# Third and fourth probability tile of thirteen attention heads turned in 32x32 blocks by VectorE and by a trip through memory, instead of by TensorE

## The chip, the cores and the metric

One core of one Trainium2 chip. The metric is device time in microseconds (us), from one launch to its end. The profile names the engines PE (TensorE, matrix products), PEld (its weight loads), DVE (VectorE), ACT (ScalarE), POOL (GpSimd) and SP (SyncE, whose queue issues most DMAs).

## The reference

Two layers of a chunk-causal encoder run over 512 prompt tokens and, with the same weights, over 64 sample tokens that also read 128 cached positions. Layer 0 has 8 heads of latent attention (heads 0 to 7 of the kernel) and 8 heads of differential attention (heads 8 to 15: two softmax maps, the second subtracted with a learned factor). Layer 1 has 8 heads of sparse attention over selected keys (heads 16 to 23). A SwiGLU follows each layer. What matters for the change is the last line of each attention:

```
p = jax.nn.softmax(logits, axis=-1)
attn = (p[:, 0] - lam * p[:, 1]).astype(v.dtype)
return jnp.einsum('bhqk,bkhd->bqhd', attn, v)
```

The softmax needs the queries on partitions and the keys along the free axis; the product with the values contracts over keys, so each tile of probabilities has to be turned until its keys lie on partitions.

## The kernel before, in words

Everything is float32, split into a high part (float32r, made by ScalarE with a Copy) and a low part (source minus high part, made by VectorE or POOL); each product is done as high x high, high x low, low x high. Each engine has an instruction stream of its own, written out by hand; the streams meet at semaphores, and a small planner only numbers the events. An attention head is eight slots, s = 0 to 7. In slots 0 to 4 TensorE makes the scores of the five query tiles t = 0 to 4 (tile t < 4 has 128 rows and 128(t+1) keys, tile 4 is the sample group), DVE adds the bias and takes the row maxima (`row_maxima`), ACT exponentiates (`exponents`, L2335) and scales (`scale_probs`, L2343), and in heads 8 to 15 DVE mixes the two maps (`mix_maps`, L3083) in the slot after. In slots 2 to 6 the tile s-2 is turned:

- `turn_probs` (L1712, L1715) on TensorE: t+1 transposes of 128x128 against the identity into one of two PSUM halves T;
- `turned_hi` (L2351) on ACT: high part from PSUM into PTh;
- `turned_lo` (L3090) on DVE: low part into PTl, which frees the PSUM half.

`weighted_values(h)` (L1724 to L1731) reads PTh and PTl of head h in slot 1 of head h+1. All other TensorE work of the slots is filler from other heads: projections of the head after (L1444 with XGh, XGl) and output products of finished heads (L1444 with MIXh, MIXl). Odd heads 9 to 15 carry eight output tiles, and end later; heads 22 and 23 have no projections left, so that head 22 is short.

The order of POOL's stream at the end of a head is: slot 4, low part of the values (Vl) and in odd sparse heads of an output (MIXl, L3652); slot 5, low part of the next keys (Kl, L3652); slot 6, a DMA of cached values (L3735), four DMAs of bias (`load_bias`, L3717, not in heads 14, 15, 22, 23), in sparse heads low part of the next queries (Ql), then the low part of the weight unit begun in this slot (`begin`, L3645); slot 7, such a weight unit if one is due; and after slot 7 of heads 10, 12 and 14 the low parts of the two finished heads' outputs (two MIXl), which TensorE needs for `output_tile` of the next head's slot 0. 

The SP queue issues the loads of weight units (L1090, each waits until its buffer's low part was made), the cached keys (L1149, in slot 2, which waits for the turn of the cached keys at the end of the head before), and in slot 4 the store of the head's keys (`store_keys`, L1133: eight DMAs from KF, which DVE has transposed in 32x32 blocks, L3022) and values. At the end of layer 0 stands a norm during which TensorE has little to do.

Of the kernel before, what the change touches and what calls it, by code (L numbers as in the profile page):

```python
# [144 lines left out]
def early_output(h):  # L145


    return h - 1 if h % 2 and kind_of(h) == "dsa" else None

# [166 lines left out]
def build(nc, a, outs, scratch):  # L316
# [58 lines left out]
    def plan_attention(h):  # L375
# [5 lines left out]
        for s in range(SLOTS):  # L381
# [5 lines left out]
            if 2 <= s < 2 + TOK_TILES and (h, s) != (16, 6):  # L387
                tr.add("p", h, s - 2)
# [333 lines left out]
    with ctx:  # L722
# [103 lines left out]
        assert e <= own  # L826
        (QIh, QIl), end3 = overlay(end3, ("QIh", [P, 4, NT], F32R), ("QIl", [P, 4, NT], F32R))
# [80 lines left out]
        pt_hi = sem("pt_hi")  # L908
        b_sq, rb_sqrt = sem("b_sq"), sem("rb_sqrt")
# [115 lines left out]
        def _(sp):  # L1025
# [112 lines left out]

            def load_next(*place):
# [11 lines left out]
            def attention(h):  # L1151
                x = next_head(h)
                for s in range(SLOTS):
                    if s == 2 and h not in (7, 16) and x is not None and kind_of(x) != "mla":
                        load_cached_keys(x)
                    if s == 4 and kind_of(h) != "mla":
                        store_keys(h)
                    load_next("slot", h, s)

# [268 lines left out]
        def _(pe):  # L1428
# [289 lines left out]
            def weighted_values(h):  # L1718
                out = open_pair("pv", h)
                pe.wait_ge(t_free, tr.made("p", h, QT))  # L1720
                pe.wait_ge(job_lo, jobs.made("v", h))
                for j in range(QT):
                    for part, (v, p) in enumerate(((Vh, PTh), (Vh, PTl), (Vl, PTh))):
                        pe.matmul(out[:, j * P:SEQ], v[:, j, :], p[:, j, j * P:SEQ],  # L1724
                                  start=(j == 0 and part == 0), stop=(j == QT - 1 and part == 2), skip_group_check=True)


                for j, tile in enumerate((TOK_TILES - 1, TOK_TILES)):
                    pe.matmul(out[:, SEQ:NT + DEC], Vh[:, tile, :], PS[:, j, :, :].rearrange("p a q -> p (a q)"),
                              start=(j == 0), stop=False, skip_group_check=True)  # L1730
# [58 lines left out]
            def attention(h):  # L1789
                g, x = prepared_in(h), next_head(h)  # L1790
                for s in range(SLOTS):
# [12 lines left out]
                    if 2 <= s < 2 + TOK_TILES and (h, s) != (16, 6):  # L1804
                        turn_probs(h, s - 2)
# [396 lines left out]
        def _(act):  # L2202
# [123 lines left out]
            def exponents(h, t):  # L2326
                kind, r, w = kind_of(h), rows_of(t), keys_of(t)
                n = step_of(h, t)
                if n >= 2:
                    act.wait_ge(t_done, tr.made("p", *divmod(n - 2, TOK_TILES)))  # L2330
# [24 lines left out]

            def b_square(h):
# [11 lines left out]
            def attention(h):  # L2368
                g, x, p = prepared_in(h), next_head(h), finished_pair(h)
                for s in range(SLOTS):  # L2370
# [6 lines left out]
                    if 2 <= s < 2 + TOK_TILES and (h, s) not in ((15, 5), (16, 4)):  # L2377
                        turned_hi(h, s - 2)
                    if h in OUTPUT_FIRST and s == 2:
# [50 lines left out]
                    if h < 16 and g is not None and s == k_job_slot(g) == 5:  # L2430
                        job("k", g)
                    if s == 5 and h < 7 and h % 2 and h > 1:
# [357 lines left out]
        def _(dve):  # L2790
# [294 lines left out]

            def turned_lo(h, t):
# [71 lines left out]
            def attention(h):  # L3158
                g, x, p = prepared_in(h), next_head(h), finished_pair(h)
                for s in range(SLOTS):  # L3160
# [3 lines left out]
                    if s < TOK_TILES:  # L3164
                        row_maxima(h, s)
                    if h == 16 and s < 3:
# [12 lines left out]
                    if 2 <= s < 2 + TOK_TILES:  # L3179
# [457 lines left out]
        def _(pool):  # L3637
# [15 lines left out]

            def add_squares(norm):
# [89 lines left out]
            def attention(h):  # L3744
                g, x, p = prepared_in(h), next_head(h), finished_pair(h)
                for s in range(SLOTS):
# [282 lines left out]
```

## Time and profile before

| | us |
|---|---|
| median of 3 runs | 1643.68 |
| lowest and highest | 1642.51, 1647.01 |
| the profiled execution's own time | 1643.9 |
| its span, first to last instruction | 1642.1 |
| mean granted TensorE clock | 0.997 of full |
| HBM read, written | 130.69 MB, 15.32 MB |
| DMA packets | 283008, of them under 512 B: 60591 |

The profile comes from one execution; its own time is 0.2 us above the median of the runs, and its span leaves out 1.8 us around the first and the last instruction. Durations in groups are means in ns; a timeline row has the start in us from the span's start, the duration in us, engine, line, operation, output and inputs, count, and in brackets the idle time of the engine before it with what ended it. The heads touched begin on TensorE between 263.8 us (head 8) and 477.2 us (head 14), and between 1043.1 us (head 17) and 1201.7 us (head 22).

### The profile page before, as it was taken

Reading aid. Unit: us, or ns where it says so; the run is one execution under the profiler, and the core shown is the slowest. Engines: PE = TensorE matmul, PEld = TensorE weight load, DVE = VectorE, ACT = ScalarE, POOL = GpSimd, SP = SyncE. Lnnn points to the kernel's source line nnn. Section 1 sums busy time; section 2 is a strip of 40 time slices with the busy share of each in tenths; the row PEclk is TensorE's granted clock in tenths of the full one; section 3 lists DMA queues with packets and bytes.
Section 4 is the critical chain, followed back from the end, with each engine's and each line's share of the span. In section 5 each row is a group of like instructions: output and inputs, shape, how many; then the busy total and the mean of one; then the engine's idle time right before and its main releaser. Section 6 shows DMA issues by size and latency. Waiting matters only on the chain.

```text
span 1642.1 us, 32437 instructions
## 1 busy us (share of the span) xinstructions
PE 1612.4 (98%) x12028; PEld 1563.2 (95%) x12028; DVE 1202.8 (73%) x2233; ACT 902.5 (55%) x1776; POOL 903.1 (55%) x703
## 2 busy tenths in 40 slices
PE   9999999999999999999999999999999999999998
PEld 8989999999999999999999999899999999999997
DVE  5666655656656799889897789634357998898977
ACT  4365545454546665565565445644367655655654
POOL 4453445364544067677575547664450676775754
PEclk9999999999999999999999999999999999999999
DMA  6221223343422223423323332344242233233232
GB/s 189 81 64 53 67 78 86 77 108 77 112 75 68 65 78 92 115 71 111 97 84 90 89 81 70 92 120 110 64 110 60 78 94 112 74 107 98 84 91 71
DMA packets 283008, 145.50 MB, mean 89 GB/s; under 512 B 60591, under 2 KB 273261, under 8 KB 282853
## 3 DMA queue, kind: packets, MB, share of 16 engines
q1 hardware_dynamic: 278392, 136.27, 30.1%
q0 software_dynamic: 3616, 6.92, 1.6%
q8 instruction: 98, 1.61, 0.4%
q14 instruction: 58, 0.47, 0.1%
q10 hardware_dynamic: 844, 0.24, 0.1%
HBM read 130.69 MB, written 15.32 MB: 89 GB/s over the span
## 4 chain that ended last, share of the span: by engine, by line
PE 81%; DVE 11%; ACT 3%; issue 3%; POOL 1%; DMA 0%; POOLq 0%; ACTq 0%; DVEq 0%
PE ACC L1444 29%; PE ACC L1883 11%; PE ACC L1884 11%; PE ACC L1885 11%; PE ACC L1724 2%; PE S L1699 2%; PE S L1885 2%; PE S L1883 2%; PE S L1884 2%; DVE SCO L3137 2%; DVE TOP L3134 1%; PE T L1444 1%; ACT PR L2335 1%; PE T L1712 1%; PE S L1673 1%
## 5 line engine op out<-in xcount | busy, mean ns | idle before, releaser
L3645 POOL TENSOR_TENSOR WL<-RAW,WH 128x1024 fp32r<-128x1024 f32 (+3 forms) x89 | 187.8, 2114 | 147.2 <-ACT WH L2210 147.0
L1444 PE MATMUL ACC<-XGh,WH 128*128 128x288 f32 (+1 forms) x1008 | 227.6, 307 | 6.3 <-DVE XGl L2828 1.8
L1444 PE MATMUL ACC<-XGh,WL 128*128 128x288 f32 (+1 forms) x1008 | 215.3, 295 | 0.0
L1444 PE MATMUL ACC<-XGl,WH 128*128 128x288 f32 (+1 forms) x1008 | 215.3, 295 | 0.0
L1883 PE MATMUL ACC<-TB,WH 128*128 128x288 f32 x640 | 188.5, 295 | 1.4 <-DVE TB L3355 1.4
L1885 PE MATMUL ACC<-TB,WL 128*128 128x288 f32 x640 | 188.6, 295 | 0.0
L1884 PE MATMUL ACC<-TB,WH 128*128 128x288 f32 x640 | 188.3, 294 | 0.0
L2493 ACT ACTIVATE TC<-ACC 128x288 f32<-128x288 f32 x192 | 79.0, 411 | 167.7 <-PE ACC L1885 167.0
L1444 PEld LDWEIGHTS ACC<-XGh,WH 128*128 128x128 f32 (+1 forms) x1008 | 159.0, 188 | 11.4 <-issue 4.0
L1444 PEld LDWEIGHTS ACC<-XGh,WL 128*128 128x128 f32 (+1 forms) x1008 | 161.6, 188 | 0.0
L1444 PEld LDWEIGHTS ACC<-XGl,WH 128*128 128x128 f32 (+1 forms) x1008 | 161.3, 187 | 0.0
L2335 ACT ACTIVATE PR<-SX,STAT 128x128 f32<-128x128 f32 (+4 forms) x160 | 85.7, 536 | 119.4 <-DVE STAT L3065 117.6
L2822 DVE TENSOR_TENSOR X<-ACC,X 128x576 f32<-128x576 f32 x89 | 66.7, 753 | 83.8 <-PE ACC L1444 79.4
L2210 ACT ACTIVATE WH<-RAW 128x1024 fp32r<-128x1024 f32 (+4 forms) x127 | 116.3, 923 | 12.9 <-PE S L1444 4.5
L1883 PEld LDWEIGHTS ACC<-TB,WH 128*128 128x128 f32 x640 | 120.2, 188 | 1.8 <-issue 1.8
L3308 DVE TENSOR_TENSOR WL<-RAW,WH 128x512 fp32r<-128x512 f32 (+3 forms) x128 | 120.4, 941 | 2.0 <-ACT WH L2511 2.0
L1884 PEld LDWEIGHTS ACC<-TB,WH 128*128 128x128 f32 x640 | 120.5, 188 | 0.0
L1885 PEld LDWEIGHTS ACC<-TB,WL 128*128 128x128 f32 x640 | 120.3, 188 | 0.0
L2511 ACT ACTIVATE WH<-RAW 128x1024 fp32r<-128x1024 f32 (+3 forms) x128 | 100.5, 787 | 34.4 <-PE S L1885 34.4
L3652 POOL TENSOR_TENSOR Ql<-YQ,Qh 128x576 fp32r<-128x576 f32 x24 | 34.9, 1455 | 112.2 <-ACT Qh L2241 112.1
L2351 ACT ACTIVATE PTh<-T 128x128 fp32r<-128x128 f32 (+1 forms) x96 | 41.2, 429 | 99.1 <-PE T L1712 98.8
L1883 PE MATMUL ACC<-XGh,WH 128*128 128x288 f32 x320 | 94.3, 295 | 0.0
(517 smaller groups left out, 5244.2 us busy)
## 6 DMA issues: line engine op xcount, KB each, us to landing
RAW<-in_w_gate_dram SPq DMA_DIRECT2D x44, 512.0 KB, 3.9
RAW<-in_w_up_dram SPq DMA_DIRECT2D x44, 512.0 KB, 5.0
RAW<-in_w_down_dram SPq DMA_DIRECT2D x48, 384.0 KB, 3.8
RAW<-in_w_in_even_dram SPq DMA_DIRECT2D x29, 512.0 KB, 5.2
RAW<-in_w_in_odd_dram SPq DMA_DIRECT2D x28, 512.0 KB, 4.6
RAW<-in_w_out_even_dram SPq DMA_DIRECT2D x16, 512.0 KB, 4.2
RAW<-in_w_down_dram SPq DMA_DIRECT2D x16, 256.0 KB, 2.9
RAW<-in_w_out_odd_dram SPq DMA_DIRECT2D x8, 512.0 KB, 5.1
```

What stands on the lines that cost most here:

```text
L1444: ins = pe.matmul(out[0:m, 512 * b:512 * b + width], left, right[:, b * width:(b + 1) * width], start=(first and part == 0), stop=(last an ...
L1883: pe.matmul(out, hi[:, w], xh, start=first and k == 0, stop=False, skip_group_check=not first)
L1884: pe.matmul(out, hi[:, w], xl, start=False, stop=False, skip_group_check=not first)
L1885: ins = pe.matmul(out, lo[:, w], xh, start=False, stop=k == count - 1, skip_group_check=not first)
L2210: act.activation(WH[slot][:, 0:n], RAW[slot][:, 0:n], ACT.Copy).then_inc(w_hi, 1)
L2335: act.activation(PR[m][0:r, n % 2, 0:w], SX[m][0:r, 0:w], ACT.Exp, bias=STAT[0:r, n % 2, m:m + 1], scale=-1.0, accum_out=STAT[0:r, n % 2, ...
L2351: act.activation(PTh[:, 0:t + 1, t * P:(t + 1) * P], out[:, 0:(t + 1) * P].rearrange("p (j q) -> p j q", q=P), ACT.Copy).then_inc(pt_hi, 1)
L2493: act.activation(dst, sum_bank(j), ACT.Copy).then_inc(copy_done, 1)
L2511: act.activation(blocks_of(layer, what, w)[0], src, ACT.Copy).then_inc(s7_hi, 1)
L2822: return lambda out: dve.tensor_tensor(two(X[:, m, :]), halves(out), two(X[:, m, :]), ALU.add)
L3308: dve.tensor_tensor(lo, src, hi.bitcast(F32), ALU.subtract).then_inc(s7_lo, 1)
L3645: pool.tensor_tensor(WL[slot][:, 0:n], RAW[slot][:, 0:n], WH[slot][:, 0:n].bitcast(F32), ALU.subtract).then_inc(w_lo_pool, 1)
```

## The change

For heads 8 to 14 and 17 to 22, and for tiles t = 2 and t = 3, the three and four TensorE transposes, the ACT copy from PSUM and the DVE subtraction are left out of slots 4 and 5. In their place:

- slots 3 and 4, DVE (`probs_to_blocks`): one `transpose` of the tile, 128 x 384 or 128 x 512, within 32x32 blocks, into a buffer PB2 or PB3. ACT's `exponents` two tiles later waits for this instead of TensorE's turn.
- SP (`turn_through_memory`), after all of the head's other entries: for each tile a store of the blocks, four DMAs (one for each 32 partitions, pieces of 128 B) into the memory of the output y_prompt, which gets its values only at the end, and one DMA that reads them back with keys on partitions (pieces of 512 B) into PF2 or PF3. The order is: store tile 2, store tile 3, load tile 2 (waits for the landing of its stores), load tile 3.
- ACT (`loaded_hi`): high part from PF2 at the end of slot 5, from PF3 in slot 7 ahead of the cached keys.
- POOL (`loaded_lo`): low part of tile 2 at the end of slot 5, that of tile 3 in slot 7, ahead of the slot's `begin`, behind all of slot 6.
- TensorE's `weighted_values` also waits for the low part of tile 3.

```
+BLOCK_TILES = (2, 3)
+BLOCK_HEADS = (8, 9, 10, 11, 12, 13, 14, 17, 18, 19, 20, 21, 22)
+            def store_blocks(h, t):
+                b = BLOCK_HEADS.index(h)
+                sp.wait_ge(pb_made, block_number(h, t) + 1)
+                if b:
+                    sp.wait_ge(pf_in[t], 16 * b)
+                place, first = turned_place(t)
+                for q in range(QUADRANTS):
+                    dst = bass.AP(place, first + q * SQUARE, [[P, SQUARE], [P * SQUARE, QUADRANTS * (t + 1)], [1, SQUARE]])
+                    sp.dma_start(dst, PB[t][q * SQUARE:(q + 1) * SQUARE, 0:(t + 1) * P].rearrange(
+                        "p (b q) -> p b q", q=SQUARE)).then_inc(pb_out[t], 16)
+            def load_turned(h, t):
+                b = BLOCK_HEADS.index(h)
+                sp.wait_ge(pb_out[t], 16 * QUADRANTS * (b + 1))
+                if b:
+                    sp.wait_ge(pf_lo, block_number(BLOCK_HEADS[b - 1], t) + 1)
+                place, first = turned_place(t)
+                src = bass.AP(place, first, [[P, P], [P * P, t + 1], [1, P]])
+                sp.dma_start(PF[t][:, :, :], src).then_inc(pf_in[t], 16)
+            def turn_through_memory(h):
+                for t in BLOCK_TILES:
+                    store_blocks(h, t)
+                    if t > BLOCK_TILES[0]:
+                        load_turned(h, t - 1)
+                load_turned(h, BLOCK_TILES[-1])
...
+                if h in BLOCK_HEADS:
+                    turn_through_memory(h)
...
             def weighted_values(h):
                 out = open_pair("pv", h)
                 pe.wait_ge(t_free, tr.made("p", h, QT))
+                if h in BLOCK_HEADS:
+                    pe.wait_ge(pf_lo, block_number(h, BLOCK_TILES[-1]) + 1)
...
-                    if 2 <= s < 2 + TOK_TILES and (h, s) != (16, 6):
+                    if 2 <= s < 2 + TOK_TILES and (h, s) != (16, 6) and not in_blocks(h, s - 2):
                         turn_probs(h, s - 2)
...
+            def loaded_hi(h, t):
+                act.wait_ge(pf_in[t], 16 * (BLOCK_HEADS.index(h) + 1))
+                act.wait_ge(acc_done, acc.made("pv", h - 1))
+                act.activation(PTh[:, 0:t + 1, t * P:(t + 1) * P], PF[t][:, :, :],
+                               ACT.Copy).then_inc(pf_hi, 1)
...
+                    if s == 7 and h in BLOCK_HEADS:
+                        loaded_hi(h, 3)
...
+                    if s == 5 and h in BLOCK_HEADS:
+                        loaded_hi(h, 2)
...
+            def probs_to_blocks(h, t):
+                b, n = BLOCK_HEADS.index(h), step_of(h, t)
+                dve.wait_ge(*probs_made(h, t))
+                if b:
+                    dve.wait_ge(pb_out[t], 16 * QUADRANTS * b)
+                w = (t + 1) * P
+                dve.transpose(PB[t][:, 0:w], PR[0][:, n % 2, 0:w]).then_inc(pb_made, 1)
...
                         row_maxima(h, s)
+                    if s and in_blocks(h, s - 1):
+                        probs_to_blocks(h, s - 1)
...
+            def loaded_lo(h, t):
+                cols = slice(t * P, (t + 1) * P)
+                pool.wait_ge(pf_hi, block_number(h, t) + 1)
+                pool.tensor_tensor(PTl[:, 0:t + 1, cols], PF[t][:, :, :],
+                                   PTh[:, 0:t + 1, cols].bitcast(F32), ALU.subtract).then_inc(pf_lo, 1)
...
+                    if s == 7 and h in BLOCK_HEADS:
+                        loaded_lo(h, 3)
                     begin("slot", h, s)
+                    if s == 5 and h in BLOCK_HEADS:
+                        loaded_lo(h, 2)
```

## Rows read from the trace of the kernel before

**Rows 1.** part 1 of the page, busy time of each engine over the span

```profile
PE 1612.4 (98%) x12028; PEld 1563.2 (95%) x12028; DVE 1202.8 (73%) x2233; ACT 902.5 (55%) x1776; POOL 903.1 (55%) x703
```

**Rows 2.** timeline of TensorE in head 12: start us, duration us, then engine, line, operation

```profile
423.10 0.55 PE L1712 MATMUL T<-IDN,PR 128*128 128x128 f32 x3
423.40 0.52 PE L1444 MATMUL ACC<-XGh,WH 128*128 128x288 f32 x2
...
425.60 0.43 PE L1444 MATMUL ACC<-XGh,WL 128*128 128x288 f32 x2
425.87 0.60 PE L1712 MATMUL T<-IDN,PR 128*128 128x128 f32 x4
426.22 0.51 PE L1444 MATMUL ACC<-XGh,WH 128*128 128x288 f32 x2
426.57 0.42 PE L1444 MATMUL ACC<-XGl,WH 128*128 128x288 f32 x2
```

**Rows 3.** groups by line and form, POOL, VectorE, ScalarE: busy us, mean ns of one

```profile
L3645 POOL TENSOR_TENSOR WL<-RAW,WH 128x512 fp32r<-128x512 f32 x13 | 17.4, 1335 | 16.3 <-ACT WH L2210 16.3
...
L3645 POOL TENSOR_TENSOR WL<-RAW,WH 128x384 fp32r<-128x384 f32 x8 | 8.6, 1075 | 12.3 <-ACT WH L2210 12.3
...
L3022 DVE STREAM_TRANSPOSE KF<-YK 128x576 f32<-128x576 f32 x16 | 12.3, 768 | 0.0
...
L2351 ACT ACTIVATE PTh<-T 128x512 fp32r<-128x512 f32 x24 | 14.0, 583 | 3.6 <-PE T L1712 3.6
```

**Rows 4.** timeline at the end of head 12: VectorE, then POOL, then TensorE

```profile
422.87 0.75 DVE L3083 SCALAR_TENSOR_TENSOR PR<-PR,STAT,PR 128x512 f32<-128x512 f32 x1 [0.61 <-ACT PR L2343]
...
429.71 1.44 POOL L3652 TENSOR_TENSOR Kl<-YK,Kh 128x576 fp32r<-128x576 f32 x1 [0.51 <-ACT Kh L2241]
...
433.76 2.40 POOL L3645 TENSOR_TENSOR WL<-RAW,WH 128x1024 fp32r<-128x1024 f32 x1
436.11 2.81 POOL L3652 TENSOR_TENSOR MIXl<-BO,MIXh 128x576 fp32r<-128x576 f32 x2
...
439.56 0.43 PE L1444 MATMUL ACC<-MIXh,WH 128*128 128x288 f32 x2
```

**Rows 5.** store line L1133 (issue ns min/median/max), then DMA issues: KB, us to landing

```profile
L1133 SPq DMA_DIRECT2D out_dsa_k_prompt_dram<-KF x32: 344/490/2198, 1038.6 to 1220.4; - x32
...
out_dsa_k_prompt_dram<-KF SPq DMA_DIRECT2D x32, 64.0 KB, 3.0
...
RAW<-in_w_kv_up_dram SPq DMA_DIRECT2D x8, 256.0 KB, 2.7
```

**Rows 6.** timeline at the end of head 14, POOL, then TensorE in head 15

```profile
502.90 2.40 POOL L3645 TENSOR_TENSOR WL<-RAW,WH 128x1024 fp32r<-128x1024 f32 x1
...
508.65 0.53 PE L1444 MATMUL ACC<-MIXh,WH 128*128 128x288 f32 x2
```

**Rows 7.** timeline, POOL at the ends of heads 19, 21, TensorE in heads 20, 22

```profile
1135.90 2.40 POOL L3645 TENSOR_TENSOR WL<-RAW,WH 128x1024 fp32r<-128x1024 f32 x1
...
1139.45 0.47 PE L1724 MATMUL ACC<-PTh,Vh 128*128 128x512 f32 x1
...
1201.75 2.40 POOL L3645 TENSOR_TENSOR WL<-RAW,WH 128x1024 fp32r<-128x1024 f32 x1
...
1202.93 0.47 PE L1724 MATMUL ACC<-PTh,Vh 128*128 128x512 f32 x1
```

**Rows 8.** timeline of POOL at the start of head 19, idle before in brackets

```profile
1106.19 4.73 POOL L3645 TENSOR_TENSOR WL<-RAW,WH 128x1024 fp32r<-128x1024 f32 x2 [6.29 <-ACT WH L2210]
```

**Rows 9.** timeline of head 22 (ScalarE) and head 23 (TensorE)

```profile
1209.88 0.72 ACT L2343 ACTIVATE PR<-PR,STAT 128x512 f32<-128x512 f32 x1 [0.23 <-DVE STAT L3073]
...
1219.13 0.48 PE L1724 MATMUL ACC<-PTh,Vh 128*128 128x512 f32 x1
```

**Rows 10.** windows at layer 0 end: length, busy us (xcount) per engine, PEclk, DMA share, GB/s

```profile
536.00:540.00 4.00, 2.83 (x21) 2.50 (x21) 1.35 (x5) 1.11 (x4) 0.38 (x1) 0.96 0.01 2
540.00:544.00 4.00, 4.00 (x21) 4.00 (x21) 0.39 (x1) 0.91 (x1) 1.18 (x2) 0.61 0.02 4
```

More of the change, by code:

```diff
@@ L148, in early_output, with in_blocks, block_number @@
     return h - 1 if h % 2 and kind_of(h) == "dsa" else None
+BLOCK_TILES = (2, 3)
+BLOCK_HEADS = (8, 9, 10, 11, 12, 13, 14, 17, 18, 19, 20, 21, 22)
+def in_blocks(h, t):
+    return h in BLOCK_HEADS and t in BLOCK_TILES
+def block_number(h, t):
+    return BLOCK_HEADS.index(h) * len(BLOCK_TILES) + BLOCK_TILES.index(t)
 def q_job_slot(g):
@@ L826, in build @@
         assert e <= own
+        (PB2, PF2, PF3), e = overlay(e, ("PB2", [P, 3 * P], F32), ("PF2", [P, 3, P], F32), ("PF3", [P, 4, P], F32))
+        assert e <= own
+        (PB3,), e = overlay(sq_off + size([P, NT], F32), ("PB3", [P, SEQ], F32))
+        PB, PF = {2: PB2, 3: PB3}, {2: PF2, 3: PF3}
         (QIh, QIl), end3 = overlay(end3, ("QIh", [P, 4, NT], F32R), ("QIl", [P, 4, NT], F32R))
@@ L908, in build @@
         pt_hi = sem("pt_hi")
+        pb_made, pf_hi, pf_lo = (sem(n) for n in ("pb_made", "pf_hi", "pf_lo"))
+        pb_out, pf_in = ({t: sem(f"{n}{t}") for t in BLOCK_TILES} for n in ("pb_out", "pf_in"))
         b_sq, rb_sqrt = sem("b_sq"), sem("rb_sqrt")
@@ L1137, in store_keys, with turned_place @@
                 sp.dma_start(outs[dst + "_sample"][:, c], VF[0:DEC, QT, :]).then_inc(vf_out, 16)
+            def turned_place(t):
+                return outs["y_prompt"].tensor, BLOCK_TILES.index(t) * P * SEQ
+            def store_blocks(h, t):
[22 more added lines that the diff above has]
+                load_turned(h, BLOCK_TILES[-1])
             def load_next(*place):
@@ L1803, in attention @@
                         output_tile(*out_tile(h, s))
-                    if 2 <= s < 2 + TOK_TILES and (h, s) != (16, 6):
+                    if 2 <= s < 2 + TOK_TILES and (h, s) != (16, 6) and not in_blocks(h, s - 2):
                         turn_probs(h, s - 2)
@@ L2329, in exponents @@
                 if n >= 2:
-                    act.wait_ge(t_done, tr.made("p", *divmod(n - 2, TOK_TILES)))
+                    before = divmod(n - 2, TOK_TILES)
+                    if in_blocks(*before):
+                        act.wait_ge(pb_made, block_number(*before) + 1)
+                    else:
+                        act.wait_ge(t_done, tr.made("p", *before))
                 if h == 16 and t == 0:
@@ L2376, in attention @@
                         job("k", g)
-                    if 2 <= s < 2 + TOK_TILES and (h, s) not in ((15, 5), (16, 4)):
+                    if 2 <= s < 2 + TOK_TILES and (h, s) not in ((15, 5), (16, 4)) and not in_blocks(h, s - 2):
                         turned_hi(h, s - 2)
+                    if s == 7 and h in BLOCK_HEADS:
+                        loaded_hi(h, 3)
                     if h in OUTPUT_FIRST and s == 2:
@@ L3178, in attention @@
                         evacuate(("wo", *out_tile(h, s)), add_to_x(out_tile(h, s)[1]))
-                    if 2 <= s < 2 + TOK_TILES:
+                    if 2 <= s < 2 + TOK_TILES and not in_blocks(h, s - 2):
                         turned_lo(h, s - 2)
```

## The prediction, on record before the changed kernel ran

> **What bounds the kernel now.** I read the shares of busy time first: PE is busy 98% of the span, DVE 73%, POOL 55% [rows 1]. Work taken from PE is thus worth its full length wherever nobody else is late, and the shares of POOL and DVE say nothing about the ends of heads. So I went through the timelines of the thirteen heads: PE for what the turns cost [rows 2], then POOL against PE around each change of head [rows 4, 6 to 8], because there the new low parts stand in POOL's queue, and PE waits for them. What the reader is to see there: POOL's stream ends a head with a dense run, and PE needs its last results shortly after.
>
> **What PE saves.** In head 12 the three transposes of tile 2 push the next product back by 0.30 us (423.10 to 423.40), the four of tile 3 by 0.35 us (425.87 to 426.22) [rows 2]. Each pair of products takes 0.27 us (425.60 to 425.87), but the first pair after the turn 0.35 us (426.22 to 426.57). For tile 2 that 0.08 us stays, since scores stand in front of it; for tile 3 it goes. A head saves 0.73 us; thirteen save 9.5 us. That is all that the change can give: PE waits for the turned tiles nowhere for long, so no stall goes.
>
> **What DVE and ACT pay.** DVE gets one block transpose instead of one subtraction of the same width. The transpose of 576 columns is 768 ns [rows 3], so 512 take 683 and 384 take 512 ns by columns. DVE has idle time before and after in these slots, 0.61 us before the mix in rows 4, and is 73% busy: I count 0, covered by that waiting for ACT; were the cover gone, 1.2 us a head. ACT's two copies only change their source: 0 in length. But they are moved behind the trip, and what is queued behind them on ACT (turn of tile 4, high part of the next queries and weights, cached keys, first exponentials of the next head) waits with them.
>
> **The trip through memory, head 12.** The mix of tile 3 ends at 423.62 [rows 4]; its transpose ends at 424.3 at the earliest, and I take 425, as the row maxima of tile 4 stand in front. SP issues four stores: median 0.49 us each, minimum 0.34 [rows 5], so 2.0 us; it then stands at 427 and issues the load of tile 2, whose stores landed meanwhile (3.0 us for 64 KB, rows 5). The nearest load in size, 256 KB, lands after 2.7 us [rows 5]: PF2 at 429.7, high part at 430.2. POOL ends Kl at 431.15 [rows 4], so the low part of tile 2 waits for nobody, with about 1 us to spare. Tile 3: last store issued 426.5, landed 429.5, loaded by 432.2. POOL comes to it only after 437, so it has 4 us to spare. SP is past its entries by 430; two weight loads for the next head's slot 0, which stood ahead, are now issued behind the trip, and are due on ACT some 10 us later: 0, covered by that. The four issues of tile 2, 2 us, fall in SP's idle time before. Bounds for a 64 KB store or such a load: 2.7 and 3.0 us are rows for other directions and sizes; I keep 1 us less and 2 us more for the range.
>
> On the stores: 64 KB in pieces of 128 B land no sooner than 256 KB in large pieces, 3.0 against 2.7 us [rows 5]. The Trainium skill ("DMA: Bandwidth & Descriptors", Specifications) says that transfers need 512 B or more for line rate, and that below it the engine reads, modifies and writes; that speaks against this change. The trace agrees in that a quarter of the bytes is no faster. As a rule of its own it is the first rival below.
>
> **What POOL pays.** Low parts of 512 and 384 columns: 1.335 and 1.075 us, from weight units of those widths [rows 3], 2.41 us a head. Where POOL's run is dense, all that is behind ends 2.41 us later.
> - Head 12: the two MIXl end at 436.11 + 2.81 = 438.92; PE needs the second at 439.56, its product of the second finished head [rows 4]. New end 441.33: PE loses 1.77 us against before, with its own saving spent too. Head 10 repeats the pattern: 3.5 us together.
> - Head 14: Kl ends near 502.4, low part of tile 2 to about 503.5, DMA issue 0.56, then the weight unit of 2.40 (502.90 before, rows 6) ends near 506.4, tile 3 near 507.7, two MIXl of 2.81 together (rows 4) near 510.5. PE had that product at 508.65 [rows 6]: 1.9 us lost.
> - Head 19: the weight unit ends at 1135.90 + 2.40 = 1138.30, the low part of tile 3 at 1140.71; PE wants it at 1139.45 [rows 7]: 1.26 us lost. Head 17 repeats it: 2.5 us together.
> - Head 21: 1201.75 + 2.40 + 2.41 = 1206.56 against 1202.93 [rows 7]: 3.6 us lost, as slot 0 of head 22 has no filler.
> - Heads 8, 11, 13, 18 and 20: POOL has long been idle when the next head begins, as with 6.29 us before 1106.19 [rows 8], or PE comes later there; the saving stays whole, 5 x 0.73 = 3.7 us gained. In head 9 spare time and low parts are about equal: 0.
> - Head 22: here the trip itself is late. The scaling of tile 3 ends at 1210.60 [rows 9], the blocks at 1211.3. SP has the stores of tile 2 in front, then four of tile 3: until 1213.3 at 0.49 us, until 1215.7 when one takes 0.78, twice the span from minimum to median above the former [rows 5]. Last landing 1215.8 to 1217.9, load 2.7, high part 0.58 [rows 3], low part 1.34: 1220.4 to 1222.8, and PE wants it at 1219.13 [rows 9]. 1.3 to 3.7 us lost; I take 2, nearer to the median issue.
>
> Sum: 3.5 + 1.9 + 2.5 + 3.6 - 3.7 + 2 = 9.8 us lost, all savings accounted for.
>
> **The clock.** The granted clock falls once inside the work: PE is busy 2.83 of 4.00 us from 536 to 540, and the next four microseconds have a mean of 0.61, the lower of the two levels (1.2 GHz) for most of it, after 0.96 [rows 10]. That costs 4 x 0.39 + 4 x 0.04 = 1.7 us. PE's new wait in head 22 is 3.6 + 0.7 = 4.3 us in one piece, that in head 23 near 3 us, both longer than the 1.17 us idle in those four: I count a fall for each, 3.4 us. The waits of 2.0 to 2.5 us at the ends of heads 10, 12, 14, 17, 19 stand between dense products; bounds are 0 and 1.7 us each, I take 0, nearer to the rest of the trace, in which shorter gaps between dense products bring no fall.
>
> The profiled execution of before took 1643.9 us, 0.2 above the median of its runs, 1643.7. With 9.8 + 3.4 = 13.2 us: 1657.1, or 1657 against the median (+0.8%).
>
> **Rivals.**
> 1. *The trip is late everywhere.* If small stores or loads take 2 us more than the rows of other uses, the low part of tile 2 comes 1 us late on POOL in heads 10, 12, 14, 17, 19, 21, and head 22 loses 4 more (two passages): 6 + 4, with another fall or two of the clock 1669 to 1672. For it: pieces of 128 B, and eight stores in a row. Against: the key stores have the same form and land in 3.0 us [rows 5]. It decides from 1 us of lateness on. The skill's rule named above is this rival.
> 2. *The clock falls at every new wait.* Five more falls of 1.7 us: 1665.5. For it: rows 10. The Trainium skill ("TensorE: Matmul & The Clock Gate", on thin-M kernels) tells of waits between bursts that throw the array back to the lower clock; the trace agrees in the one place of rows 10.
> 3. *Not slower: POOL keeps up.* Place: POOL's run from Kl to the low part of tile 3 at the end of each head. If its later entries have slack that I don't see, or ACT's products are ready earlier so that the run moves forward by 2.4 us, PE finds everything made, and 9.5 us are saved: 1634.4. It decides from a low part that ends before PE's first product with PTh. For it: POOL is only 55% busy [rows 1]. Against: the runs have no idle time in rows 4 and 7 into which 2.41 us go. A middle form, in which half the heads wait and the clock doesn't fall, ends near 1644.
> That the change doesn't do what it says I leave out: it drops the transposes from PE's stream by name.
>
> **How the numbers follow.** Forecast case, 1650 to 1664 (head 22 by its bounds, no fall or two more): 0.55. Rival 1: 0.12. Rival 2: 0.10. Rival 3: 0.07 in full, 0.16 in its middle form, 1639 to 1650. About 0.3% (4.9 us) is what a measurement can tell from no change: 1638.8 to 1648.6. Slower: 0.55 + 0.12 + 0.10 + 0.05 of the middle form = 0.82; same 0.11; faster 0.07. The range of 1646 to 1669 leaves out rival 3, the lower half of its middle form, and the upper half of rival 1.
>
> **What will show it.** L1712 has 91 transposes fewer. PE idles before L1724 in heads 18, 20, 22 and 23, released by POOL's new low part, 2, 2, 4 and 3 us, and before L1444 with MIXh in heads 11, 13 and 15, released by POOL MIXl. ACT waits for the DMA of PF2 less than 2 us in full heads, longest in head 22. If PE has no new idle time there, the POOL step is wrong. If PE's wait ends on ACT's high part or on the DMA in full heads, the trip step is wrong. If the granted clock stays full through head 22, the clock step is. If the new POOL rows are not near 1.34 and 1.08 us, their price is.

## The result, and the profile after

The changed kernel took 1656.7 us in the median of 4 runs (1654.9 to 1658.7), the kernel before 1643.1 (1641.9 to 1647.0, 4 runs): ratio 1.0079, 95% interval 1.0061 to 1.0096. It is slower, 13.6 us by the medians, and the interval puts the loss between 10 and 16 us. Its profiled execution took 1654.9, the fastest of the four, and is 11.0 us longer than the one of before; the ledger below is of these 11.0.

The page of the changed kernel, busy time and the granted clock in 40 slices:

```profile
PE 1607.8 (97%) x11937; PEld 1555.8 (94%) x11937; DVE 1202.7 (73%) x2233; ACT 904.1 (55%) x1776; POOL 933.0 (56%) x729
PEclk9999999999999999999999999999989999999999
```

PE has 91 instructions and 4.6 us less than in [rows 1], POOL 26 and 29.9 us more, DVE the same. The span grew, so what grew is waiting. The waits of TensorE, by line and what ended them (total us, times, longest):

```profile
PE ACC L1783 <- POOL PTl L3742: 8.5, 4, 4.7
PE ACC L1501 <- DVE X L2895: 4.0, 6, 2.1
PE ACC L1501 <- POOL MIXl L3736: 3.1, 6, 1.1
PE T L1772 <- DVE PR L3156: 2.0, 4, 1.1
```

All four are new or longer. Line 3742 is POOL's new low part, 3736 the low part of a finished head's output, 2895 the sum of an output tile into x, 1772 the turn of the sample tile, which stays on TensorE. The new instructions, groups by form (busy us, mean ns):

```profile
L3742 POOL TENSOR_TENSOR PTl<-PF,PTh 128x512 fp32r<-128x512 f32 x13 | 16.7, 1283 | 0.0
L3742 POOL TENSOR_TENSOR PTl<-PF,PTh 128x384 fp32r<-128x384 f32 x13 | 13.2, 1015 | 1.4 <-ACT PTh L2422 1.4
...
L2422 ACT ACTIVATE PTh<-PF 128x384 fp32r<-128x384 f32 x13 | 6.8, 526 | 21.5 <-DMA PF<-out_y_prompt_dram 21.4
...
L3166 DVE STREAM_TRANSPOSE PB<-PR 128x512 f32<-128x512 f32 x13 | 9.1, 699 | 0.5 <-ACT PR L2406 0.5
L3166 DVE STREAM_TRANSPOSE PB<-PR 128x384 f32<-128x384 f32 x13 | 7.5, 574 | 0.0
```

One low part of each width is 2.30 us a head (forecast 2.41). The block transposes are 0.70 and 0.57 (forecast 0.68 and 0.51). ACT stood 21.4 us for tile 2 to come back from memory, over thirteen heads: 2.07 to 3.64 us in heads 9, 17, 19, 21 and 22, longest in head 21, less than 1.9 in the others. The issues and landings of the trip, from the DMA part:

```profile
out_y_prompt_dram<-PB SPq DMA_DIRECT2D x52, 64.0 KB, 1.9
...
PF<-out_y_prompt_dram SPq DMA_DIRECT2D x13, 256.0 KB, 2.9
```

64 KB in pieces of 128 B landed in 1.9 us, sooner than the 3.0 us of the key stores in [rows 5].

**Head 12 into 13**, answering to [rows 4]: POOL, then TensorE.

```profile
428.19 1.43 POOL L3736 TENSOR_TENSOR Kl<-YK,Kh 128x576 fp32r<-128x576 f32 x1
429.59 1.01 POOL L3742 TENSOR_TENSOR PTl<-PF,PTh 128x384 fp32r<-128x384 f32 x1
...
435.56 1.28 POOL L3742 TENSOR_TENSOR PTl<-PF,PTh 128x512 fp32r<-128x512 f32 x1
436.80 2.79 POOL L3736 TENSOR_TENSOR MIXl<-BO,MIXh 128x576 fp32r<-128x576 f32 x2
...
404.98 0.33 PE L1730 MATMUL S<-Kh,Qh 64*128 64x128 f32 x2
...
426.67 0.41 PE L1772 MATMUL T<-IDN,PR 128*128 128x128 f32 x2 [0.28 <-DVE PR L3156]
...
438.36 0.50 PE L1501 MATMUL ACC<-MIXh,WH 128*128 128x288 f32 x2 [0.62 <-POOL MIXl L3736]
439.64 0.53 PE L1501 MATMUL ACC<-MIXh,WH 128*128 128x288 f32 x2 [0.26 <-POOL MIXl L3736]
```

Of the turns in [rows 2] nothing is left: PE is 0.30 us ahead after the first and 0.71 after the second and the pair behind it. The head begins at 404.98, 0.97 earlier than before (405.95). Counted from the head's start, the low part of the keys begins after 23.21 us, before after 23.76: PE had saved its turns by then, and the keys came earlier. Behind it POOL has the two new low parts, and the two MIXl end after 34.61 instead of 32.97. PE takes the second after 34.66, before after 33.61. The row of 426.67 is the other thing to see: PE, 0.7 us ahead after both missing turns, waits for VectorE's mix of the sample tile. That mix and POOL beside it, then the same mix in the kernel before:

```profile
424.99 1.54 DVE L3156 SCALAR_TENSOR_TENSOR PR<-PR,STAT,PR 64x192 f32<-64x192 f32 x1 [0.35 <-ACT PR L2406]
...
423.92 2.39 POOL L3729 TENSOR_TENSOR WL<-RAW,WH 128x1024 fp32r<-128x1024 f32 x1
...
426.33 1.16 DVE L3083 SCALAR_TENSOR_TENSOR PR<-PR,STAT,PR 64x192 f32<-64x192 f32 x1 [0.35 <-ACT PR L2343]
```

Such a mix took 0.40 or 0.41 us in five of the eight heads. In heads 10, 12 and 14 it ended 0.21 us after POOL's weight unit, and took 1.53 or 1.54 us (1.15 or 1.16 before). Counted from the start of head 12, VectorE began it after 20.01 us instead of 20.38, and it ended after 21.55 where before it ended after 21.54: with POOL's weight unit both times.

**Heads 19, 21 and 22**, answering to [rows 7] and [rows 9]: POOL and PE at the end of head 19, then ACT, POOL and PE at the end of 21.

```profile
1140.07 1.27 POOL L3742 TENSOR_TENSOR PTl<-PF,PTh 128x512 fp32r<-128x512 f32 x1
...
1141.59 0.47 PE L1783 MATMUL ACC<-PTh,Vh 128*128 128x512 f32 x1 [1.84 <-POOL PTl L3742]
...
1199.01 0.53 ACT L2422 ACTIVATE PTh<-PF 128x384 fp32r<-128x384 f32 x1 [3.64 <-DMA PF<-out_y_prompt_dram]
...
1199.62 1.02 POOL L3742 TENSOR_TENSOR PTl<-PF,PTh 128x384 fp32r<-128x384 f32 x1 [0.70 <-ACT PTh L2422]
...
1206.92 1.25 POOL L3742 TENSOR_TENSOR PTl<-PF,PTh 128x512 fp32r<-128x512 f32 x1
...
1208.52 0.77 PE L1783 MATMUL ACC<-PTh,Vh 128*128 128x512 f32 x1 [4.73 <-POOL PTl L3742]
```

In both heads the product with PTh starts 0.25 to 0.35 us after the low part of tile 3 ends. In head 21 two things come together: PE has 4.73 us of nothing, and ACT got tile 2 late (3.64 us of waiting), which made POOL idle for 0.70 us ahead of its dense run. At the end of head 22 (SP, ACT, DVE, then PE in head 23):

```profile
1216.71 4.07 SPq L1173 DMA_DIRECT2D out_y_prompt_dram<-PB  x8
1220.88 1.74 SPq L1183 DMA_DIRECT2D PF<-out_y_prompt_dram  x2
...
1223.78 0.52 ACT L2422 ACTIVATE PTh<-PF 128x384 fp32r<-128x384 f32 x1 [2.25 <-DMA PF<-out_y_prompt_dram]
1224.21 0.26 ACT L2417 ACTIVATE PS<-T 128x128 fp32r<-128x128 f32 x1
...
1224.50 0.29 DVE L3175 TENSOR_TENSOR PS<-T,PS 128x128 fp32r<-128x128 f32 x1 [4.40 <-ACT PS L2417]
1224.71 0.75 DVE L2895 TENSOR_TENSOR X<-ACC,X 128x576 f32<-128x576 f32 x1
...
1225.51 0.53 PE L1501 MATMUL ACC<-MIXh,WH 128*128 128x288 f32 x2 [2.12 <-DVE X L2895]
```

The eight stores leave SP in 4.07 us. ACT stands at tile 2 until 1223.78; behind it on ACT is the high part of the sample tile (PS), behind that on DVE its low part, and behind that the sum into x that PE's next product waits for.

**The clock**, answering to [rows 10] (windows of 4 us: PE busy, ..., granted clock, DMA share, GB/s):

```profile
508.00:512.00 4.00, 3.75 (x20) 3.01 (x20) 1.59 (x4) 2.83 (x7) 1.87 (x2) 0.66 0.03 4
...
1204.00:1208.00 4.00, 0.00 (x0) 0.00 (x0) 1.44 (x6) 1.87 (x6) 4.00 (x3) 0.70 0.53 83
1208.00:1212.00 4.00, 3.48 (x12) 3.24 (x13) 0.00 (x0) 0.00 (x0) 0.17 (x1) 0.50 0.71 204
...
1224.00:1228.00 4.00, 2.49 (x12) 2.50 (x13) 2.76 (x7) 1.26 (x4) 3.98 (x4) 0.76 0.56 181
```

Three stretches have the lower level (1.2 GHz) in them, each during or behind a new wait: 1.34 us (in two pieces) in head 15, 4.73 in head 22, 2.12 in head 23. The fall of [rows 10] is missing in this execution, though TensorE waits 1.17 us at that place here too. So it does in all twelve profiled executions of this case, and the fall is there in three of them: before, run 2 and run 7. Run 5 keeps the old turn and has no fall either, and other executions of the kernel before were granted 0.997 to 1.000 of the full clock. So I take its absence as scatter and not as an effect of the change; that isn't shown.

**The ledger**, from the starts of PE's instructions in both traces, head by head (us against before; a wait counts where PE waits):

| | measured | forecast |
|---|---|---|
| gain of heads 8, 11, 13, 18, 20 | -3.6 | -3.7 |
| head 9 (saving given back to the sample tile's mix, then 0.5 in head 10's waits, its own low part among them) | +0.5 | 0 |
| heads 10 and 12, each with the MIXl wait in the next head | +0.9, +0.95 | +1.75 each |
| head 14 | +1.1 | +1.9 |
| heads 17 and 19 | +1.2, +1.26 | +1.26 each |
| head 21, with its wait in head 22 | +4.2 | +3.6 |
| head 22, with its wait in head 23 | +1.8 | +2 |
| lower clock: heads 15, 22, 23, less the missing fall | +1.5, +1.8, +1.6, -1.5 | 3.4 |
| start of the program, ahead of head 8 (-0.9 to +5.4 in the runs below: scatter) | -0.9 | 0 |
| sum (the spans: 10.8) | +10.8 | +13.2 |

### The profile page after: what moved, and what is told of

It reads as the page before. It is cut to its first block, busy times and chain, and to the rows that moved or that the text cites. A ratio compares the mean times of both kernels' runs of the same rounds, so it can differ in the third digit from the quotient of the medians.

```text
span 1652.9 us, 32470 instructions
## 1 busy us (share of the span) xinstructions
PE 1607.8 (97%) x11937; PEld 1555.8 (94%) x11937; DVE 1202.7 (73%) x2233; ACT 904.1 (55%) x1776; POOL 933.0 (56%) x729
## 4 chain that ended last, share of the span: by engine, by line
PE 73%; DVE 11%; POOL 6%; ACT 4%; issue 3%; DMA 2%; SPq 1%; POOLq 0%; ACTq 0%; DVEq 0%
PE ACC L1501 23%; PE ACC L1942 11%; PE ACC L1943 11%; PE ACC L1944 11%; PE ACC L1783 3%; POOL WL L3729 2%; PE S L1944 2%; PE S L1942 2%; PE S L1943 2%; PE S L1756 2%; DVE SCO L3219 2%; ACT PR L2398 1%; DVE TOP L3216 1%; PE T L1501 1%; POOL PTl L3742 1%
## 5 line engine op out<-in xcount | busy, mean ns | idle before, releaser
L1944 PE MATMUL ACC<-XGh,WL 128*128 128x288 f32 x320 | 94.3, 295 | 0.0
```

The lines of the kernel that those rows point to most:

```text
L1944: ins = pe.matmul(out, lo[:, w], xh, start=False, stop=k == count - 1, skip_group_check=not first)
```

## The experiments

**Theories.** A: low parts on POOL end its dense runs later, and PE waits there; trip and VectorE lie beside other work. B: the trip itself (its latency, or its traffic) is the price. C: TensorE's clock is. Ten kernels. A ratio goes against the kernel before in the same session. The changed kernel is in none of these sessions, so where I set a run against its 1656.7, I also give what is left when each is taken against its own kernel before (the changed kernel: 13.6 us longer, by its interval 10 to 16).

**1. Without heads 21 and 22.**

```
-BLOCK_HEADS = (8, 9, 10, 11, 12, 13, 14, 17, 18, 19, 20, 21, 22)
+BLOCK_HEADS = (8, 9, 10, 11, 12, 13, 14, 17, 18, 19, 20)
```

> Heads 21 and 22 turn all tiles on TensorE again, the other eleven heads as in the change. My theory: most of the loss sits at the end of head 21 (POOL's low part of tile 3 behind its weight unit, PE 4.7 us idle, the clock at its lower level) and in the short head 22 (the trip is late): 1647 to 1648.5 us, no PE wait over 1 us after 1200 us that before did not have, clock at full there. Rival, a cost spread evenly over all heads (DMA traffic, DVE, SP): eleven thirteenths of the loss stay, 1654.5 us.

Measured 1645.9 us (11 runs), ratio 1.0017 (1.0009 to 1.0026). That is 3.2 us above before instead of 13.6, so two heads carry some 10.4 us, more than I had expected (1647 to 1648.5). No wait of PE over 1 us is left after 1200 us, and the clock is full there.

**2. Only heads 8, 11, 13, 18, 20**, those in which the forecast found POOL idle (`BLOCK_HEADS` cut to them).

> Only heads 8, 11, 13, 18 and 20 go through memory, those at whose end POOL is idle long before TensorE needs it. My theory: each saves its 0.73 us, 1639.5 us (1638 to 1641), faster than both kernels. Rival, a cost spread over all heads: 1645 or more. Rival, TensorE's saving is eaten by other waits within the head: 1643.

Measured 1639.4 us (8 runs), ratio 0.9972 (0.9962 to 0.9983): faster than both. By intervals (from the start of a head to the start of the next, against before) the five heads give 0.89, 0.67, 0.67, 0.72 and 0.70 us, and no wait of PE for POOL's low parts is in the trace. The 0.73 us a head are real; whether they are kept is decided at the end of the head. The interval of head 8 is the least certain: it is 0.23 longer in run 5.

**3. Low part of tile 3 earlier in POOL's order.**

```
+                        if h in BLOCK_HEADS:
+                            loaded_lo(h, 3)
                         if h >= 16 and g is not None:
                             job("q", g)
...
-                    if s == 7 and h in BLOCK_HEADS:
-                        loaded_lo(h, 3)
```

> As the change, but POOL makes the low part of tile 3 in slot 6, ahead of the next queries and of slot 6's weight unit, instead of in slot 7 behind them. Nothing else moves, the trip is as long as before. My theory (POOL's order decides): PE's waits before the first product with PTh in heads 18 and 20 (1.7 and 1.8 us) go, that in head 22 shrinks from 4.7 to about 1 us with the lower clock there gone or shorter; the MIXl waits of heads 11, 13, 15 stay as they are: 1646 to 1650 us. Rival (the trip through memory is late): these waits stay and now end on ACT's high part, 1656 us.

Measured 1643.9 us (11 runs), ratio 1.0005 (0.9997 to 1.0014). The same work in another order is 12.8 us shorter (1.2 us above its own before, so 12.3 shorter). PE's waits for it (total, times, longest), then POOL and PE at the end of head 21:

```profile
PE ACC L1783 <- POOL PTl L3742: 1.8, 2, 1.1
...
1198.96 1.28 POOL L3742 TENSOR_TENSOR PTl<-PF,PTh 128x512 fp32r<-128x512 f32 x1
1200.19 1.42 POOL L3736 TENSOR_TENSOR Ql<-YQ,Qh 128x576 fp32r<-128x576 f32 x1
...
1200.59 0.47 PE L1783 MATMUL ACC<-PTh,Vh 128*128 128x512 f32 x1 [1.15 <-POOL PTl L3742]
```

The product needs PTl 1.15 us after it would like to, not 4.73, and the next queries and weights, now behind, still come in time. The waits of heads 18 and 20 are gone, so all of their loss was the order. What is left stands in heads 22 and 23, 1.11 and 2.42 us longer than before: this 1.15, and 1.63 for the X sum behind ACT's wait; and in heads 11, 13 and 15, whose waits for MIXl stay as expected (0.89, 0.88 and 1.53 us), since the order moved nothing out from in front of MIXl. The total is below the range that I had expected (1646 to 1650).

**4. No trip:** DVE writes its blocks into the buffers that the loads filled, so tiles 2 and 3 are turned only within blocks, and stores and loads are gone.

```
-                    dve.wait_ge(pb_out[t], 16 * QUADRANTS * b)
+                    dve.wait_ge(pf_lo, block_number(BLOCK_HEADS[b - 1], t) + 1)
...
-                dve.transpose(PB[t][:, 0:w], PR[0][:, n % 2, 0:w]).then_inc(pb_made, 1)
+                dve.transpose(PF[t][:, :, :].rearrange("p a b -> p (a b)"), PR[0][:, n % 2, 0:w]).then_inc(pb_made, 1)
```

> As the change, but the stores and loads are left out: DVE writes its blocks straight into PF2 and PF3 (so tiles 2 and 3 of the probabilities stay turned only within blocks), and ACT's high parts wait for DVE alone. My theory: POOL's queue is as long as in the change, so the waits of heads 18 and 20 and the MIXl waits stay, that of head 22 is 4 us with the lower clock; only head 22's own lateness goes in part (ACT is not held up, the 2.1 us wait on the X update in head 23 is gone, but POOL's low part of tile 3 then stands behind Kl, Vl and a weight unit): 1651 to 1654 us. Rival (the trip is the cost): all waits gone, 1634 to 1640 us.

Measured 1654.9 us (5 runs), ratio 1.0063 (1.0048 to 1.0077), just above the range expected. It is 12.2 us above its own before where the changed kernel is 13.6 above: latency and traffic of the trip together are worth 1 to 2 us by the medians, which the intervals don't tell from nothing. The waits stand where they stood:

```profile
1074.53 0.47 PE L1781 MATMUL ACC<-PTh,Vh 128*128 128x512 f32 x1 [1.52 <-POOL PTl L3740]
...
1206.80 0.47 PE L1781 MATMUL ACC<-PTh,Vh 128*128 128x512 f32 x1 [3.90 <-POOL PTl L3740]
...
1227.14 0.47 PE L1781 MATMUL ACC<-PTh,Vh 128*128 128x512 f32 x1 [2.39 <-POOL PTl L3740]
```

3.90 instead of 4.73 us in head 22, so the trip's lateness there is 0.8; and in head 23, where the X sum now is early, PE waits 2.39 us for POOL instead. That wait was hidden behind the other, and with the clock behind it head 23 is 1.9 us longer than in the changed kernel. Small shares of the trip show in other heads: the waits in heads 18 and 20 are 1.52 and 1.58 instead of 1.73 and 1.84, and the wait for the low part in head 10 (0.25) is gone.

**5. The trip beside the old turn.** Block transposes, stores and loads stay, and nothing reads what comes back; the turn on TensorE with its copies is back.

```
-            if 2 <= s < 2 + TOK_TILES and (h, s) != (16, 6) and not in_blocks(h, s - 2):
+            if 2 <= s < 2 + TOK_TILES and (h, s) != (16, 6):
...
-                    if s == 7 and h in BLOCK_HEADS:
-                        loaded_hi(h, 3)
...
-                    if s == 5 and h in BLOCK_HEADS:
-                        loaded_lo(h, 2)
```

> The block transposes, the stores to memory and the loads of all thirteen heads stay as the change has them; the old turn on TensorE, its copies on ScalarE and VectorE stay too, and the values that come back from memory are not used (nothing is added on Pool). This prices the trip by itself, beside other work. Theory (the time is lost by the low parts on Pool, the trip costs nothing where nobody waits for it): between 1641 and 1646 us, within 0.2% of before, and no new wait of TensorE. Rival (the traffic of 128-byte pieces, or VectorE's 1.3 us more a head, holds other work up): 1648 us or more, with TensorE or ScalarE seen to wait for transfers or for VectorE.

Measured 1642.45 us (11 runs), ratio 1.0001 (0.9992 to 1.0010). 104 stores, 26 loads and 16.6 us of block transposes cost nothing that the medians show beside the rest; by intervals heads 8, 9 and 22 are 0.1 to 0.2 us longer, the others within 0.03. Queue 1 in the DMA part of its page (packets, MB, share of 16 engines):

```profile
q1 hardware_dynamic: 338712, 148.20, 33.5%
```

Before, that queue had 278392 packets, 136.27 MB and 30.1%. 60320 packets more took 3.4% of 16 x 1640 us, 15 ns each, at 198 B on average; those of before took 28 ns at 489 B.

**6 and 9. TensorE kept busy through its wait** at the end of head 21, by 38 and by 19 products of ones into the bank that the weighted sum then overwrites (work added, output unchanged).

```
+                if h == 21:
+                    for _ in range(38):
+                        pe.matmul(out[:, 0:P], ONES[:, :], ONES[:, :], start=True, stop=True)
                 if h in BLOCK_HEADS:
```

> The change, with 38 products of a 128x128 tile of ones put in front of head 21's weighted sum, into the bank that the weighted sum then overwrites (work added that changes nothing in the output). They fill the time in which TensorE waits for the low part of tile 3 (4.73 us in the trace of the changed kernel), so the wait itself is not shorter. Theory (a part of the loss in heads 22 and 23 is TensorE's clock, which falls behind that wait and stays at the lower level for 6.8 us of head 22): the clock stays at 1.00 there, head 22 is 2.5 to 3.5 us shorter, the total 1652.5 to 1654.5 us. Rival (the clock falls for another reason, or what TensorE loses is not what the end waits for): 1656 to 1657.5 us. Should the products take longer than the wait, each 0.1 us beyond it is lost again.

With 38: 1655.0 us (5 runs), ratio 1.0073 (1.0060 to 1.0087). That is between the ranges of theory and rival. A product of ones took 0.23 us, so that they ran on well past the wait: POOL's low part was ready at 1207.73, and the weighted sum began at 1211.66. The clock is full in heads 22 and 23. The total is 1.7 below the changed kernel's, but 12.8 us above its own before against 13.6, and the intervals overlap: this run shows no gain. So the run with 19:

> As the run with 38 products of ones ahead of head 21's weighted sum, with 19 of them. There one such product took 0.23 us (76 instructions, 8.75 us), so that they filled the wait and 3.1 us more, and the total was still 1.7 us below the changed kernel's. 19 take 4.4 us, about the length of the wait. Theory (TensorE's lower clock behind the wait is a part of the loss): the clock is full in heads 22 and 23, head 22 is 3 to 5 us shorter than in the changed kernel, the total 1651.5 to 1653.5 us. Rival (the gain in the run with 38 was chance, since head 22 itself was longer there): 1655.5 to 1657.5 us.

1652.6 us (5 runs), ratio 1.0061 (1.0048 to 1.0074), 4.0 below the changed kernel (10.3 us above its own before, so 3.3; the intervals just overlap). Its windows in heads 22 and 23:

```profile
1204.00:1208.00 4.00, 3.88 (x32) 3.59 (x31) 0.86 (x3) 1.13 (x4) 3.22 (x2) 1.00 0.44 95
...
1220.00:1224.00 4.00, 1.18 (x10) 1.04 (x9) 1.84 (x5) 1.49 (x4) 3.98 (x5) 1.00 0.75 246
1224.00:1228.00 4.00, 4.00 (x20) 3.77 (x20) 2.84 (x10) 2.39 (x6) 2.03 (x2) 0.57 0.50 84
```

The clock is full through head 22 now, and that head is 1.95 us shorter than in the changed kernel (3 to 5 expected: the lower level costs 1.8 there, as the ledger has it); behind the next wait, PE busy 1.18 of 4 us, it falls again. So "full in heads 22 and 23" was wrong for 23. That next wait is 2.82 us here instead of 2.12, and head 23 is 0.74 longer than in the changed kernel, so 1.2 us are left of the 1.95 over both heads. In the profiled executions the rest of the difference is head 15, 1.5 us shorter because its fall is missing, which the products don't touch; the medians I can't place. The clock in head 22 is a consequence of the wait, worth about 2 us there, not the wait itself.

**7. Seven heads with the earlier order:** the edit of 3, and

```
+BLOCK_HEADS = (8, 11, 13, 17, 18, 19, 20)
```

> The low part of tile 3 moved up in Pool's order, ahead of the next queries' and weights' low parts (as in the run with that order), and only heads 8, 11, 13, 17, 18, 19 and 20 turned in blocks. By the intervals of the two earlier runs (covered heads alone, and low part earlier) each of these gains 0.65 to 0.9 us: 8 0.9, 11 and 13 0.67 each, 17 0.75, 18 and 20 0.7 each, 19 0.8, in all 5.2. Theory (the gains add, since each head's wait is its own): 1637.0 to 1638.5 us, below both kernels and below the run of five heads (1639.4). Rival (Pool's work of neighbouring heads 17 to 20 adds up, and the last of them, or head 21, pays): 1639.5 to 1642 us, with a wait for Pool in heads 19 to 22.

Measured 1638.0 us (1637.6 to 1638.5, 6 runs), ratio 0.9971 (0.9960 to 0.9983). By intervals the seven give 0.76, 0.71, 0.68, 0.73, 0.70, 0.81 and 0.69 us, 5.1 together, and none waits. It is below both kernels; that it is below run 2 is seen in the intervals of heads 17 and 19, but the ratios overlap.

**8. Low part of tile 2 on VectorE**, at the start of slot 7 (first hunk: VectorE's stream, second: POOL's). The semaphore `pf_lo` becomes one for each tile, and TensorE and the loads wait for them.

```
+                    if s == 7 and h in BLOCK_HEADS:
+                        loaded_lo(h, 2)
...
-                    if s == 5 and h in BLOCK_HEADS:
-                        loaded_lo(h, 2)
```

> The change with the low part of tile 2 (128x384) on VectorE, at the start of slot 7, instead of on Pool; Pool keeps tile 3's. Pool is 1.0 us a head less busy, VectorE 0.5 us more, in a stretch in which it waits for TensorE. Theory (Pool's queue sets the end of the heads that wait): the waits of 1.7 to 1.8 us at the ends of heads 18 and 20 shrink to about 0.8, the waits of some 0.6 and 1.1 us for the mixed values in heads 10, 12 and 14 vanish or nearly, head 22's wait loses at most 1.0 (the trip is late there too); total 1648 to 1652 us. Rival (the trip through memory or ScalarE's high part sets the end): 1655 to 1657 us, the waits unchanged. Third way (VectorE's added work delays the next values or scores): over 1657 us.

Measured 1656.7 us (5 runs), ratio 1.0086 (1.0071 to 1.0100). Its profiled execution is the slowest of the five, 1661.6; 5.4 us of that lie ahead of head 8, and I compare heads. No gain, and both the theory and the third way happened. POOL's share is as theory A has it: heads 18 and 20, 1.3 and 1.4 us longer than before in the changed kernel, are 0.13 and 0.19 longer here, and the wait in head 22 is 2.96. But heads 11 and 13 are 3.5 us longer than before each (0.5 in the changed kernel). VectorE and POOL at the end of head 10, VectorE at the end of head 20, PE:

```profile
365.96 4.67 DVE L3174 TENSOR_TENSOR PTl<-PF,PTh 128x384 fp32r<-128x384 f32 x1
...
366.60 2.39 POOL L3740 TENSOR_TENSOR WL<-RAW,WH 128x1024 fp32r<-128x1024 f32 x1
368.93 1.28 POOL L3753 TENSOR_TENSOR PTl<-PF,PTh 128x512 fp32r<-128x512 f32 x1
370.16 1.73 POOL L3747 TENSOR_TENSOR MIXl<-BO,MIXh 128x576 fp32r<-128x576 f32 x1
...
1143.06 0.55 DVE L3174 TENSOR_TENSOR PTl<-PF,PTh 128x384 fp32r<-128x384 f32 x1
...
372.27 0.53 PE L1502 MATMUL ACC<-XGh,WH 128*128 128x288 f32 x2 [2.75 <-DVE BO L3205]
```

The first subtraction took 4.67 us and the second 0.55. The second met only DMA issues on POOL. The first met POOL's weight unit and its low part of tile 3, and ended at 370.63, 0.42 us after that low part (370.21), while POOL's next, MIXl, was stretched from its usual 1.43 to 1.73. It had begun 0.64 us before the weight unit, longer than the 0.55 it takes alone; what held it in those 0.64 us, in which POOL only issued DMAs, stays open. Of the thirteen subtractions five met only DMA issues, four of them took 0.55 and one 1.02; the other eight ended 0.41 to 0.43 us after an elementwise instruction of POOL, and took 0.94 to 4.69. Behind it stands what PE waits for. The block transposes are not touched by this: 0.57 and 0.70 us on average in every kernel with the change, none more than 0.015 from it, though in the changed kernel twelve of the 26 ran beside an elementwise instruction of POOL. No run varies POOL's work under a fixed VectorE instruction; what shows the cause is that all eight late ends follow POOL's. The Trainium skill ("GPSIMD Engine Reference", 1. Specifications) has it that GpSimd shares its SBUF interfaces with VectorE, and that they contend where VectorE's instruction reads two inputs from SBUF. The trace agrees: this subtraction reads two (PF and PTh), and took up to 4.69 us; the transpose reads one, and kept its time.

**10. Without head 22.**

> The change for twelve heads, without head 22. With neither 21 nor 22 it was 1645.9 us, with both 1656.7. Theory (head 21's turn takes the time of head 22: its low part of tile 3 comes late, TensorE waits 4.7 us and then has the lower clock; head 22's own turn takes that of head 23, where ScalarE stands at tile 2's values and the output tile's sum comes late): head 22 is 5.5 to 6.5 us longer than before, head 23 to the end as before or up to 0.5 us longer, total 1652 to 1653.5 us. Rival (head 22's stores and loads also press on head 22): head 22 only 2 to 4 us longer, total 1648 to 1650 us. Other rival (head 23 is long only because head 22 began it late): head 23 stays 2 to 4 us longer, total 1655 us or more.

Measured 1652.3 us (5 runs), ratio 1.0058 (1.0044 to 1.0072). Head 22 is 6.45 us longer than before, head 23 to the end 0.28: head 21's turn is paid in head 22, head 22's in 23. Taking 22 away saves 4.4 us, then 21 6.4 (3.7 and 6.7, each against its own before).

## Why the prediction was right, point by point

The forecast was 1657 and the median is 1656.7. It is right by its reason and partly by luck in the sum. The sum was 13.2 us; the pair of profiled executions shows 10.8, the medians 13.6, and their interval reaches from 10 to 16. Within the 10.8, too much for heads 10, 12 and 14 (2.4 us) stands against too little for heads 9 and 21 (1.1), and an unforeseen fall of the clock (1.5) against one that happened to be missing (1.5); 0.9 is scatter at the start of the program.

- **PE's saving, 0.73 a head:** right where nobody waits, 0.65 to 0.9 (runs 2 and 7).
- **DVE, 0 us:** its own cost is 0 (run 5), but the step missed something. In heads 10, 12 and 14 TensorE, 0.7 us ahead, waits for VectorE's mix of the sample tile and gives back 0.45; in head 9 it gives back all of it (1.15 us at line 1772, 0.32 before). That chain was just in time before, so a faster PE gained nothing from it. What holds it is POOL: in heads 10, 12 and 14 the mix ends 0.21 us after POOL's weight unit, and in head 9 the mix of tile 3 in front of it is stretched to 2.35 us in the same way. This is read from the trace; no run takes that weight unit away. The cover I named (waiting for ACT) hides VectorE's cost, and doesn't make its result earlier.
- **The trip:** in full heads beside other work, nearly as said: run 5 for traffic, run 4 for latency. The claim that tile 2's low part waits for nobody failed in head 21 (POOL idle 0.70 us), and for less in heads 9 (0.53) and 19 (0.22). My sign "ACT waits less than 2 us in full heads, longest in head 22" failed too: 2.07, 2.16, 3.16 and 3.64 in heads 9, 17, 19 and 21. For head 22 the place was wrong: I had the low part of tile 3 as the end, and it was the X sum, through ACT's wait for tile 2; I had counted ACT's queue behind the trip as covered. The amount, 1.9 against 2, is near since a wait for POOL's low part stood right behind it (2.39 us in run 4). Its upper bound is 1222.5 by its own terms (1217.9 + 2.7 + 0.58 + 1.34), not 1222.8.
- **POOL:** the price held (2.30 against 2.41). Heads 17 and 19 came out to 0.06 us. For heads 10, 12 and 14 I had 0.8 us too much each: I left the run where it was, while the keys, and so the run, came 0.55 earlier. Head 21 was 0.6 too low, by the 0.70 above.
- **The clock, 3.4:** 1.8 and 1.6 measured in heads 22 and 23. The waits of 1.73 and 1.84 us in heads 18 and 20 brought no fall, as said, and the shorter ones in head 15 did in this execution, not in those of runs 1, 3, 4, 6, 9 and 10, which have nearly the same wait there. Over all profiled executions here, a fall came with each of the nine new waits of 2.1 us and more, and with two of 31 between 1.1 and 2.1. The forecast took the fall of [rows 10] as what a wait of 1.17 us does; that same wait brought it in three of twelve executions. In the sum the fall of head 15 cancels against the missing one.
- **Rivals:** 1 (trip late everywhere) fell with runs 4 and 5; its upper end is some 1670.5 by its own terms (1657.1 + 10 + two falls of 1.7), not 1672. The rule of the Trainium skill behind it ("DMA: Bandwidth & Descriptors", Specifications: 512 B or more for line rate) agrees with run 5 in that the small pieces were slower by the byte, 13 against 17 B per ns of an engine; nobody waited for the bytes. 2 (a fall at every new wait) fell. 3 (POOL keeps up) holds in five heads, and with the order of run 3 in heads 9, 17 and 19 as well; TensorE still waits for POOL at the ends of 10, 12, 14, 21 and 22.

What stays open: why a fall of the clock comes behind the 1.34 us of head 15 in one execution and not in six others, and what the medians of run 9 gained beside head 22. Untested: whether heads 9, 10, 12 and 14 keep their saving when POOL's weight unit doesn't stand beside the sample tile's mix.

## What to carry to other kernels

An engine that is 56% busy over the span can be full at the end of each head; price added work there, and ask which entry of its queue somebody is waiting for, since the same entries in another order were worth some 12 us. Do the exchange only where the engine has idle time behind it: five or seven heads gained 3.3 and 4.2 us where thirteen lost 13.6. Time saved on the bounding engine is kept only up to the next result that was just in time, here VectorE's mix.

## What I had not expected of the hardware

A mix of the changed kernel in head 9 (VectorE), and what POOL did at the time:

```profile
321.13 2.35 DVE L3156 SCALAR_TENSOR_TENSOR PR<-PR,STAT,PR 128x512 f32<-128x512 f32 x1
...
320.54 2.40 POOL L3729 TENSOR_TENSOR WL<-RAW,WH 128x1024 fp32r<-128x1024 f32 x1
```

- A subtraction on VectorE with two SBUF inputs ended 0.41 to 0.43 us after the end of POOL's elementwise instruction in all eight cases in which it met one: 0.55 us without one, up to 4.69 with. Block transposes, with one input, kept their 0.57 and 0.70.
- VectorE's mix of 128x512, two inputs as well, took 0.75 us in five heads and 2.35 in heads 9, 11 and 13, where it began within POOL's weight unit and ended 0.54 us after it. It did so before too (2.34 to 2.38): the trace that the prediction was made from had this effect, and I didn't read it. The sample tile's mix of 64x192 took 0.40 us alone and 1.54 beside POOL in heads 10, 12 and 14.
- 64 KB in pieces of 128 B landed in 1.9 us here and in 3.0 us as key stores of the kernel before, both in the median.
